# Latent attention with its weights scaled before they are turned, and a recurrent stage whose denominators come with its outputs

## The reference

```python
scores = (jnp.einsum('bqhd,bkhd->bhqk', qn, k_nope)
          + jnp.einsum('bqhr,bkr->bhqk', qr, k_rope)).astype(jnp.float32) * scale
mask = k_idx[None, :] <= q_idx[:, None]
scores = jnp.where(mask, scores, -jnp.inf)
p = jax.nn.softmax(scores, axis=-1).astype(v.dtype)
return jnp.einsum('bhqk,bkhd->bqhd', p, v)      # then merge_blocks(o) @ w_out
```

```python
d = jnp.exp(log_d - m_t[..., None])
s = jnp.einsum('bhtk,bhsk->bhts', qc, kc) * d
num = jnp.einsum('bhts,bhsv->bhtv', s, vc) + ...
den = jnp.sum(s, axis=-1) + ...
h = num / jnp.maximum(jnp.abs(den), jnp.exp(-m_t))[..., None]
```

## Time and profile before

| | us |
|---|---|
| median of 3 runs | 1592.76 (1591.43 to 1592.95) |
| the profiled execution | 1590.94 |
| its span, first to last instruction | 1589.2 |
| PE busy in it | 1570.0, 99% |
| DVE busy | 1077.0, 68% |
| ACT busy | 787.6, 50% |
| mean granted TensorE clock | 0.999 |

### The profile page before, as it was taken

The page is one execution under the profiler, slowest core; times in us unless marked ns, Lnnn a source line. Parts: engine busy times, 40 slices in busy tenths (PEclk is TensorE's granted clock), DMA queues, the critical chain, the costliest instruction groups (busy, mean ns, idle before and its releaser), DMA issues.

```text
span 1589.2 us, 20826 instructions
## 1 busy us (share of the span) xinstructions
PE 1570.0 (99%) x8668; PEld 1354.2 (85%) x8668; DVE 1077.0 (68%) x1251; ACT 787.6 (50%) x999; POOL 37.2 (2%) x99
## 2 busy tenths in 40 slices
PE   8999999999999999999999999999999999999998
PEld 7888888788888888889888888888888878888887
DVE  6667657776666766676776665678666775876666
ACT  6444546664346444478644445435444447454443
POOL 2000000000000000000000001000000021000000
PEclk9999999999999999999999999999999999999999
DMA  8655444465554755432565554447655462565551
GB/s 301 217 188 191 151 146 133 154 222 193 186 185 146 239 185 186 160 137 79 187 223 187 192 165 133 159 151 246 203 193 203 152 221 90 175 235 187 187 195 49
DMA packets 188068, 283.35 MB, mean 178 GB/s; under 512 B 5775, under 2 KB 142598, under 8 KB 187846
## 3 DMA queue, kind: packets, MB, share of 16 engines
q1 hardware_dynamic: 184736, 271.24, 51.1%
q0 software_dynamic: 3120, 10.73, 2.0%
q10 hardware_dynamic: 118, 0.05, 0.0%
HBM read 280.46 MB, written 1.05 MB: 177 GB/s over the span
## 4 chain that ended last, share of the span: by engine, by line
PE 89%; DVE 7%; ACT 2%; issue 1%; DMA 1%; DVEq 0%; ACTq 0%
PE wk L738 24%; PE wk L741 12%; PE acc L656 9%; PE acc L657 9%; PE acc L658 9%; PE acc L707 3%; PE acc L708 3%; PE acc L711 3%; PE acc L769 2%; PE acc L759 2%; PE acc L760 2%; PE wk L656 2%; PE wk L658 2%; PE wk L657 2%; DVE weights_low L1948 2%
## 5 line engine op out<-in xcount | busy, mean ns | idle before, releaser
L1948 DVE TENSOR_TENSOR weights_low<-weights_raw,weights_high 128x2048 fp32r<-128x2048 f32 (+1 forms) x189 | 428.4, 2269 | 183.4 <-ACT weights_high L1511 182.8
L1511 ACT ACTIVATE weights_high<-weights_raw 128x2048 fp32r<-128x2048 f32 (+2 forms) x190 | 360.5, 1900 | 361.1 <-PE wk L741 214.7
L738 PE MATMUL wk<-turned_halves,weights_high 128*128 128x512 f32 x1632 | 407.5, 392 | 0.0
L738 PEld LDWEIGHTS wk<-turned_halves,weights_high 128*128 128x128 f32 x1632 | 297.5, 189 | 56.0
L656 PE MATMUL acc<-weights_high,hidden_high 128*128 128x512 f32 x640 | 250.5, 391 | 0.3 <-DVE turned_halves L2192 0.3
L657 PE MATMUL acc<-weights_low,hidden_high 128*128 128x512 f32 x640 | 249.9, 391 | 0.0
L658 PE MATMUL acc<-weights_high,hidden_low 128*128 128x512 f32 x640 | 249.1, 389 | 0.0
L741 PEld LDWEIGHTS wk<-turned_halves,weights_low 128*128 128x128 f32 x1632 | 222.6, 190 | 15.9
L741 PE MATMUL wk<-turned_halves,weights_low 128*128 128x256 f32 x1632 | 227.5, 282 | 0.0
L1511 ACT ACTIVATE weights_high<-work 128x2048 fp32r<-128x2048 f32 x66 | 126.9, 1922 | 119.2 <-PE wk L741 93.9
L1948 DVE TENSOR_TENSOR weights_low<-work,weights_high 128x2048 fp32r<-128x2048 f32 x66 | 151.3, 2292 | 45.2 <-ACT weights_high L1511 43.8
(11 more groups left out here) (378 smaller groups left out, 1871.3 us busy)
## 6 DMA issues: line engine op xcount, KB each, us to landing
weights_raw<-ffn_w_in_dram SPq DMA_DIRECT2D x76, 1024.0 KB, 5.1
work<-ffn_w_out_dram SPq DMA_DIRECT2D x28, 1024.0 KB, 4.9
weights_raw<-mlp_w_up_dram SPq DMA_DIRECT2D x22, 1024.0 KB, 5.3
weights_raw<-mlp_w_down_dram SPq DMA_DIRECT2D x22, 1024.0 KB, 4.8
weights_raw<-ffn_w_out_dram SPq DMA_DIRECT2D x16, 1024.0 KB, 4.9
weights_raw<-sb_w_in_dram SPq DMA_DIRECT2D x12, 1024.0 KB, 5.2
weights_raw<-a_w_in_dram SPq DMA_DIRECT2D x12, 1024.0 KB, 5.2
work<-ffn_w_in_dram SPq DMA_DIRECT2D x11, 1024.0 KB, 5.1
```

The source lines that it names most:

```text
L738: nc.tensor.matmul(both.rearrange("p (c s) -> p c s", c=2), wh[:, k, c], xT[:, :, k, :], start=k == 0, stop=False, skip_group_check=True)
L1511: A(part(whi, u), part(raw, u), ACT.Copy).then_inc(high_ready, 1)
L1948: V.tensor_tensor(part(wlo, u), part(raw, u), part(whi, u).bitcast(F32), ALU.subtract).then_inc(unit_ready, 1)
```

## The change

1. Latent attention: DVE scales each head's weights by the reciprocals of their sums before PE turns them (`reciprocals`). ACT copies the turned weights into one of four buffers in `work` (`mla_pT`). For two heads at a time (`chunk`), the values are the operand that stays in the array, and the turned weights stream through it: four matmuls with 64 outputs each, the second head's beside the first one's. What comes out is a chunk of the turned output, so that `turn_half` goes, for this stage, and ACT's and DVE's `keep_mixed` with it. DVE makes high and low halves of each chunk (`keep_chunk`). The first tile of the output product stands ahead of the last chunk. DVE's low halves of U+7 and U+8 stand behind `keep_chunk(7)`.
2. Recurrent stage: the values get a column of minus ones (`ML_VW` = 257) so that the denominators are the last column of the outputs; every head's output has its own bank; the product with U+8 goes to `acc[:, 0, BANK:]`, and the four spreading matmuls stand between its products; DVE splits U+9 earlier; areas move.
3. Sliding-window stage: the first half is turned one head earlier, ACT keeps one of its banks, DVE the other, after its loop.

```diff
-            return acc[:, t, h * M_DV:(h + 1) * M_DV] if h < 2 else wk[:, h, t * M_DV:(t + 1) * M_DV]
-
-        def ml_den(p):
-
-            if p == 0:
-                return wk[:, 0:2, QB:QB + T]
-            return acc[:, 0, BANK:BANK + 2 * T].rearrange("p (h t) -> p h t", t=T)
+            at = BANK * (h // 2)
+            return wk[:, 2 * (h // 2) + t, 0:ML_VW] if h % 2 else acc[:, t, at:at + ML_VW]
...
-        MIXED_AT = {"mla": 0, "mlstm": 2 * T, "swa": 4 * T}
+        MIXED_AT = {"mlstm": 0, "swa": 2 * T}
+        MIX_TURNED_AT = {"mlstm": 0, "swa": KD // 2}
+        mla_pT = work[:, 0:4 * QB].rearrange("p (b n) -> p b n", n=QB)
+
+        def mla_chunk(p):
+
+            return acc[:, p % 2, BANK:BANK + S]
...
                     wait_unit(U + c)
                     if name == "mlstm" and c:
-                        pe.wait_ge(ml["den_read"], 2)
+                        pe.wait_ge(ml["out_read"], 1)
                     for t in range(T):
+                        if name == "mla" and c == 0 and t == 0:
+                            continue
+                        if name == "mla" and c:
+                            pe.wait_ge(mla_s["chunk_kept"], PAIRS - 1 + t)
                         mm = row_tile(U + c, acc[:, t, c * BANK:(c + 1) * BANK], 0, t, BANK)
                         if t == T - 1:
                             mm.then_inc(unit_done, 1)
-                        if (c, t) == ((1, 0) if name == "mlstm" else (0, 1)):
+                        if (name, c, t) in (("mlstm", 1, 0), ("swa", 0, 1)):
                             turn_half(name, 1)
                 for t in range(T):
...
+                def chunk(p):
+
+                    pe.wait_ge(sm["probs_kept"], 2 * p + 2)
+                    if p == 0:
+                        pe.wait_ge(sm["v_kept"], 2)
+                    if p >= 2:
+                        pe.wait_ge(sm["chunk_kept"], p - 1)
+                    heads = [(mla_chunk(p)[HD * e:HD * e + HD, :], mla_pT[:, (2 * p + e) % 4, :], (2 * p + e) * HD) for e in range(2)]
+                    for o, w, at in heads:
+                        nc.tensor.matmul(o[:, 0:S], mla_v[:, 0, at:at + HD], w[:, 0:S], start=True, stop=False,
+                                         skip_group_check=True)
+                    for o, w, at in heads:
+                        mm = nc.tensor.matmul(o[:, P:S], mla_v[:, 1, at:at + HD], w[:, S:QB], start=False, stop=True,
+                                              skip_group_check=True)
+                    mm.then_inc(sm["chunk_ready"], 1)
+
...
                     turn_probs(h)
+                    if not late:
+                        if h and h % 2 == 0:
+                            chunk(h // 2 - 1)
+                        continue
                     if h:
                         values(h - 1)
-                    if late and h == 4:
+                    if h == 4:
                         turn_late()
-                    if h == HEADS - 3:
+                    if h == HEADS - 4:
                         turn_half(name, 0)
-                values(HEADS - 1)
+                if late:
+                    values(HEADS - 1)
+                    return
+                mix_fresh[0] = 0
+                wait_unit(out_unit)
+                row_tile(out_unit, acc[:, 0, 0:BANK], 0, 0, BANK)
+                chunk(PAIRS - 1)
...
                 mm.then_inc(ml["cols_turned"], 1)
-                for h in range(M_HEADS):
-                    mm = nc.tensor.matmul(wk[:, 1 + h // 2, (h % 2) * S:(h % 2 + 1) * S],
-                                          ml_select[:, h * P:(h + 1) * P], ML_M, start=True, stop=True)
-                    if h % 2:
-                        mm.then_inc(ml["spread"], 1)
-                pe.wait_ge(ml["cols_kept"], 1)
-                group_up(U + 8, 3)
+                pe.wait_ge(ml["o_kept"], T)
+                wait_unit(U + 8)
+                wh, wl = slot(whi, U + 8, 8), slot(wlo, U + 8, 8)
+                for half in range(2):
+                    c = slice(half * P, (half + 1) * P)
+                    for k in range(KD):
+                        mm = product(acc[:, 0, BANK + half * S:BANK + (half + 1) * S], (wh[:, k, c], wl[:, k, c]),
+                                     (xTh[:, k, :], xTl[:, k, :]), k == 0, k == KD - 1)
+                        if half and k == KD - 1:
+                            mm.then_inc(unit_done, 1)
+                        if k % 4 == 2:
+                            h = 2 * half + k // 4
+                            mm = nc.tensor.matmul(wk[:, 1 + h // 2, (h % 2) * S:(h % 2 + 1) * S],
+                                                  ml_select[:, h * P:(h + 1) * P], ML_M, start=True, stop=True)
+                            if h % 2:
+                                mm.then_inc(ml["spread"], 1)
...
                     pe.wait_ge(ml["weights_ready"], h + 1)
                     w = ml_scores[:, h, :]
-                    for rhs, dst in ((lambda t: ml_v[:, t, h * M_DV:(h + 1) * M_DV], lambda t: ml_out(h, t)),
-                                     (lambda t: neg_ones[:, 0:1], lambda t: ml_den(h // 2)[:, h % 2, t:t + 1])):
-                        nc.tensor.matmul(dst(0), w[:, 0:P], rhs(0), start=True, stop=True)
-                        nc.tensor.matmul(dst(1), w[:, P:S], rhs(0), start=True, stop=False)
-                        mm = nc.tensor.matmul(dst(1), w[:, S:QB], rhs(1), start=False, stop=True)
-                    mm.then_inc(ml["out_ready"], 1)
+                    nc.tensor.matmul(ml_out(h, 0), w[:, 0:P], ml_v[:, 0, h, :], start=True, stop=True)
+                    nc.tensor.matmul(ml_out(h, 1), w[:, P:S], ml_v[:, 0, h, :], start=True, stop=False)
+                    nc.tensor.matmul(ml_out(h, 1), w[:, S:QB], ml_v[:, 1, h, :], start=False,
+                                     stop=True).then_inc(ml["out_ready"], 1)
...
                     act.wait_ge(sm["probs_turned"], h + 1)
+                    if not sink:
+                        if h >= 4:
+                            act.wait_ge(sm["chunk_ready"], h // 2 - 1)
+                        A(mla_pT[:, h % 4, :], wk[:, 2 + h % 2, 0:QB], ACT.Copy).then_inc(sm["probs_kept"], 1)
+                        return
                     if h >= 2:
...
+                def reciprocals(h):
+
+                    dve.wait_ge(sm["exp_ready"], h + 1)
+                    n = slice(2 * h, 2 * h + 2)
+                    V.reciprocal(att_stat[:, RECIP, n], att_stat[:, SUMS, n]).then_inc(sm["sum_read"], 1)
+                    dve.wait_ge(sm["sum_read"], h + 1)
+                    for t, c in ((0, slice(0, P)), (1, slice(P, QB))):
+                        e, at = raised("mla", h)[:, c], 2 * h + t
+                        ins = V.tensor_scalar(e, e, att_stat[:, RECIP, at:at + 1], None, ALU.mult)
+                    ins.then_inc(sm["probs_ready"], 1)
+
+                def keep_chunk(p):
+
+                    dve.wait_ge(sm["chunk_ready"], p + 1)
+                    V.tensor_copy(xTh[:, p, :], mla_chunk(p)).then_inc(sm["chunk_high"], 1)
+                    dve.wait_ge(sm["chunk_high"], p + 1)
+                    V.tensor_tensor(xTl[:, p, :], mla_chunk(p), xTh[:, p, :].bitcast(F32),
+                                    ALU.subtract).then_inc(sm["chunk_kept"], 1)
+
                 def outputs(c):
...
                         split_half(U + 6, h // 6)
+                    if not sink and h:
+                        reciprocals(h - 1)
+                    if not sink and h >= 4 and h % 2 == 0:
+                        keep_chunk((h - 4) // 2)
                     if sink and h == 7:
                         dve.wait_ge(sm["fill_ready"], 5)
                         V.tensor_copy(swa_qT[:, 6:8, :], acc[:, 1, BANK:D].rearrange("p (e s) -> p e s", e=2)).then_inc(sm["fill_v"], 1)
                     if h in (7, 15) and sink:
                         sink_terms(h // 8)
-                    if h == 11:
+                    if sink and h == 11:
                         outputs(0)
-                keep_mixed(name, o, range(2))
+                if not sink:
+                    reciprocals(HEADS - 1)
+                    keep_chunk(PAIRS - 2)
+                    keep_chunk(PAIRS - 1)
+                    split_to(U + STAGE_UNITS[name])
+                    return
+                keep_mixed(name, o, range(1))
+                dve.wait_ge(mix_turned, MIX_TURNED_AT[name] + 2)
+                V.tensor_copy(xTh[:, 2:4, :].rearrange("p k s -> p (k s)"), mix_bank(name, 1)).then_inc(mix_high, 1)
+                keep_mixed(name, o, range(1, 2))
                 outputs(1)
...
                 V.tensor_copy(ml_small[:, 32:48], wk[:, 3, 0:16]).then_inc(ml["cols_kept"], 1)
+                split_to(U + 10)
...
                     js = range(4 * p, 4 * p + 4)
                     for j in js:
-                        chain.count(V.bn_stats(ml_small[:, 48 + 6 * j:54 + 6 * j], ml_out(j // T, j % T)))
```

(7 more changed lines are left out.)

73 lines of the change are left out of this document (40 added, 33 removed).

## The result

The changed kernel takes 1594.91 us (median of 22 runs, 1594.0 to 1595.43), the kernel before 1592.13 in the same comparison (22 runs, 1591.13 to 1593.0): a ratio of 1.0018 with a 95% interval of 1.0012 to 1.0024. It is **slower by 2.8 us**, where 1.3 us less was forecast.

What follows compares the result with a forecast made beforehand. PE was taken to bound the kernel (busy 99% of the span), VectorE the changed latent loop. Latent +2.1, recurrent -3.2 and sliding-window -0.2 us sum to -1.3: 1591.5 us against the median of 1592.76, range 1586.3 to 1596.0.

Steps and rivals of the forecast that it cites:

- PE's side of the latent stage: Latent attention: narrow value matmuls and no half turns gain PE about 6 us, if PE keeps the bound.
- outer bound of -6.3: Latent attention: the whole PE gain of about -6.3 us comes out if VectorE's scaling is hidden.
- VectorE's side: Latent attention: with the added work a pair of heads costs VectorE 3.24 us; attention in all +1.7 us.
- VectorE becomes the bound of the loop: Latent loop: VectorE sets the pace, 3.32 to 3.4 us a pair; the loop ends 3.1 us later.
- Rival C: Latent loop or exit dearer: round trip between engines, 3.9 us a pair; 1596 to 1600 us; chance 0.13.
- A: Whole kernel, terms as summed: 1591.5 us, or 1589.5 to 1594.5 with the sizes of its terms; chance 0.55.
- The exit: Latent stage's end: low halves of U+7 and U+8 start 4.4 us later; +0.4 us, range 0 to +2.
- The spreading matmuls: Recurrent stage: with the four placed between ordinary matmuls the clock stays up, -1.5 us, zero as the other bound.
- each change between the two kinds I take at the 0.1: Recurrent stage: each change between spreading and ordinary matmuls costs 0.1 us; four of them, +0.4 us.
- The one-column matmuls: Recurrent stage: each of four heads loses three one-column matmuls, 0.59 us a head, -2.36 us.
- The sliding window: Sliding-window stage: half of PE's 0.88 us wait for exponentials goes at one head; -0.2 us, from -0.9 to +0.2.
- The clock: Recurrent stage: clock does not go by PE's busy time; rival that it falls all the same, 1593 us, chance 0.10.

Runs made afterwards that it cites:

- e4: The changed kernel with VectorE's keeping of a chunk one head later, behind the scaling of an even head: ratio 1.0020 to the kernel before.
- e6: The changed kernel with chunks ahead of an odd head's turns, kept one head later, high halves written by ScalarE: ratio 1.0013 to the kernel before.
- e9: e6 with another order at the latent exit, U+7 and U+8 split earlier around the last chunk's halves: ratio 0.9991 to the kernel before.
- e13: The kernel before with only the four spreading matmuls placed between the products of U+8: ratio 1.0000 to the kernel before.
- e8: The kernel before once more, unchanged, profiled for its granted clock; no time or ratio given.
- e14: The kernel before with only the ones column and the sliding-window part, spreading matmuls still in a row: ratio 0.9991 to the kernel before.
- e15: e9 with the four spreading matmuls in a row ahead of the product: ratio 0.9987 to the kernel before.
- e2: The changed kernel with the latent attention's part undone: ratio 0.9992 to the kernel before, -1.3 us.
- e5: The changed kernel with each chunk's matmuls ahead of the turns of an odd head: ratio 1.0042 to the kernel before, +7 us.
- e11: e9 with spreading matmuls in a row and, at the recurrent exit, VectorE's low half behind the first norm: ratio 0.9991 to the kernel before.
- e12: e11 with the latent attention of the kernel before: ratio 0.9990 to the kernel before.
- e3: The changed kernel with the four spreading matmuls in a row ahead of the product again: ratio 1.0010 to the kernel before.

## Why the prediction was wrong

The forecast was 1591.5, a gain of 1.3 us; measured was a loss of 2.8. The range of 1586.3 to 1596.0 holds the 1594.91, the direction is wrong. In the traces the sum is missed by some 4.6 us (+3.35 instead of -1.3): 3.0 in the recurrent stage, 1.6 in the latent one. **Three steps failed**: the gain of the one-column matmuls taken whole (2.0 us), the bound of the latent loop (most of 1.6) and the price of the interleaving (1.0). By its steps:

- *PE's side of the latent stage*: right in the main. 0.80 us for a chunk, no turns of halves. Entering and leaving the narrow form costs 0.25 us for each chunk, against the 0.1 that was taken and left out of the 2.88; PE's own pair is 3.01. (The forecast's outer bound of -6.3 is 6.1 by its own terms, 3.5 + 1.7 + 0.9; nothing else hangs on it.) The Trainium skill's rule on changing the tiling mode ("TensorEngine Tiling (Array Packing)", Key Properties), taken as a full drain each time, would have asked more: the 0.3 us for an edge that the forecast set beside it would be 0.6 for each chunk, and the rows show 0.15 ahead of it and 0.10 behind it.
- *VectorE's side*: the prices were right (3.30 against 3.24 summed) and the bound was not. **This step failed**: "VectorE becomes the bound of the loop". I set the sum of one engine against the sum of the other and a piece of the chain (2.10 against 2.02) between them, and added 0.08. The chain that closes on itself over two heads is 3.60 long. A pair took 3.60 instead of 3.32 to 3.4. e4 showed idle time of VectorE at the same 3.60, so neither engine's own work sets it; in e6 and e9, where the chunk leaves the chain and ScalarE takes a part of VectorE's work, a pair is 3.0. That PE would wait some 0.4 us for each pair was right. Rival C named the round trip and priced it at 3.9. It is 3.6, between A and C.
- *The exit*: the mechanism was right, and +0.4 was measured as +0.7. e6 and e9 showed it to be worth over 2 us once PE comes earlier.
- *The spreading matmuls*: that the clock would stay was right in all nine profiles. That it would fall without it was taken from one trace, and came in six of nine. **This term failed**: "each change between the two kinds I take at the 0.1": 0.36 for each stretch. The gain of 1.1 became 0.05 in the traces (9.45 against 9.50), and e13's time agrees: 1.0 us of the miss.
- *The one-column matmuls*: **the dearest step that failed**, 2.0 us of the miss. -2.36 was near the truth on PE's own row (2.7), and wrong as a gain. It was taken whole by the forecast's first rule, "a saving counts if it shortens PE's own row of instructions", since PE was busy 99% of the time. But VectorE's row from the stage's turns over the second normalization, two low halves and a transfer to the next norm has no slack, since PE waited already 0.15 us for it before. It takes 21.6 to 21.8 us in before, e8 and e13 and 22.0 to 22.3 in the changed kernel, e9, e14 and e15. What PE saves behind the stage's turns comes back as the wait at 1077. The four reads of denominators cost twice: the wait of 0.54 at 1047.39 is unchanged, but PE's turns ahead of it start later, so that the way from the product's second matmul to the outputs behind the wait is 7.16 us (1042.95 to 1050.11) instead of 6.85 (1040.54 to 1047.39), 0.31 where 0.25 was forecast, and they lengthen VectorE's row to the exit as well.
- *The sliding window*: -0.2, measured -0.19.
- *The clock*: The Trainium skill ("TensorE: Matmul & The Clock Gate", Part 1) ties it to how busy PE has been. The falls behind the row came with PE busy throughout, so the traces still do not agree with that by busy time as the profile counts it; those at 1078 in the changed kernel and at 1074 in e14 came behind a wait of 1.7 to 2.1 us and do, though nine of fourteen profiles with such a wait have no fall. No term of the forecast held these second ones.

Whether the falls behind the row depend on the work or on the moment is not settled: the same instructions gave both, and each kernel has one profile (the kernel before two). The same holds for e2 and e14, whose clock fell behind a wait of 0.88 in an unchanged latent stage (in e2 0.57 in the 4 us from 754).

The mean clock of each execution says how often falls come at all, though not where. One fall takes 1.7 us of clock, 0.001 of the mean; profiles that read 1.000 hold none, those that read 0.998 or less hold one or two, and 0.999 occurs with one and with none. The kernel before reads 0.998 or less in 86 of 117 executions and 1.000 in one. e13, which differs from it by the interleaving alone, reads 0.998 or less in none of 11, the kernel before beside it in 23 of 33. So the fall that the forecast read from one trace comes in most executions of the kernel before, and the interleaving takes it away; it costs as much. The changed kernel reads 1.000 in 12 of 22 executions and 0.998 in 9, with medians of 1595.1 and 1594.7: its own falls, such as the one at 1078, show no cost.

## To carry to other kernels

Where two engines hand work back and forth, follow one datum round until the chain closes and add that up, over as many heads as it takes; neither engine's own sum shows it, and moving one end of a handover without the other can cost more than it saves. Before a saving on the busiest engine is counted, look at the next place where it waits at all: a wait of 0.15 us there meant that another engine's row ended at the same time, and most of what was saved behind that row's start was lost. A cost seen in one profile (a fall of the clock) is a chance, not a term, until others show how often it comes.

## What the runs showed of the hardware

- A stretch of matmuls with 4 partitions and plain 32-bit operands within a product of split ones costs 0.33 to 0.36 us beside its own work, whether it holds one or two of them.
- The granted clock fell to half for about 3.4 us behind four such matmuls in six of nine executions, with PE busy throughout, and never behind one or two of them in nine.
- At the recurrent stage's exit it also fell behind waits of 1.5 to 2.1 us, in 5 of the 14 profiles that have one (after, e5, e11, e12, e14; not e3 or e9, for example), in the old latent stage behind the wait of 0.88 in 2 of 6, and in e5's latent stage behind one of 1.72. Every fall was of the same length, 1.7 us of clock. It costs 1.5 to 1.7 us, or nothing where PE would wait for weights just behind it.
- Four narrow matmuls with 64 outputs among full-width ones cost 0.15 us on entering and 0.10 on leaving, beside their own 0.80.
- From VectorE's freeing of a raw slot to ScalarE's start on the next unit passed 5.2 to 5.6 us in these stretches (761.10 + 2.2 to 768.67 is 5.3), so a late low half is felt 5 us behind it, on another engine.
